# Decoder trunk on one core: gate and up slabs multiplied in two passes of 256 tokens

## The reference

```python
def swiglu(x, w_gu, w_down):
    g, u = jnp.split(x @ w_gu, 2, axis=-1)
    return (jax.nn.silu(g) * u) @ w_down

for l in range(DEPTH):          # DEPTH = 2
    x = layer_norm(ALPHA * x + 0.5 * swiglu(x, ffn1_w_gu[l], ffn1_w_down[l]), ...)
    mix = hybrid_mixer(x, positions, w_in[l], ...)   # attention, mLSTM, short convolution
    x = layer_norm(ALPHA * x + mix, ...)
    x = layer_norm(ALPHA * x + 0.5 * swiglu(x, ffn2_w_gu[l], ffn2_w_down[l]), ...)
```

## Time and profile before

| | |
|---|---|
| time, median of 2 runs | 2545.62 us (2545.02 to 2546.22) |
| span of the profiled execution | 2544.7 us |
| PE busy | 2515.7 us (99%) |
| weight loads (PEld) busy | 2053.7 us (81%) |
| DVE, ACT, POOL busy | 1131.2, 973.2, 217.8 us |
| TensorE clock granted, mean | 0.993 of full speed |
| moved by DMA | 229 MB, 90 GB/s |

### The profile page before, as it was taken

One profiled execution on the slowest core, in us unless ns is written; L12 is line 12 of the kernel. 1 busy time (PEld: TensorE's weight loads), 2 busy tenths in 40 slices (PEclk: granted clock), 3 DMA queues, 4 the chain that ended last, 5 costly groups with the idle time before them and its releaser, 6 DMA issues.

```text
span 2544.7 us, 31255 instructions
## 1 busy us (share of the span) xinstructions
PE 2515.7 (99%) x11378; PEld 2053.7 (81%) x11378; DVE 1131.2 (44%) x1584; ACT 973.2 (38%) x1334; POOL 217.8 (9%) x136
## 2 busy tenths in 40 slices
PE   8999999999999999999999999999999999999997
PEld 7888877778888778888788888787788887888886
DVE  3333344455555653333433333544455547433335
ACT  4443233344343354432344432424344433544323
POOL 0002120000000310001200021200000003000012
PEclk9999999999999999999999999989999999999999
DMA  5233232222222222322233323222222232332232
GB/s 166 90 98 99 92 88 75 77 73 83 83 83 83 96 81 89 97 95 92 95 100 99 97 92 101 55 92 67 83 83 83 68 98 83 99 99 89 90 107 79
DMA packets 229324, 229.05 MB, mean 90 GB/s; under 512 B 9440, under 2 KB 220640, under 8 KB 229216
## 3 DMA queue, kind: packets, MB, share of 16 engines
q1 hardware_dynamic: 229216, 227.66, 28.1%
HBM read 225.53 MB, written 2.10 MB: 89 GB/s over the span
## 4 chain that ended last, share of the span: by engine, by line
PE 95%; issue 2%; DVE 2%; POOL 1%; ACT 0%; DMA 0%; DVEq 0%; POOLq 0%; SPq 0%
PE main L1341 29%; PE main L1345 29%; PE main L1342 29%; PE side L1555 1%; PE side L1430 1%; DVE x L972 1%; DVE xl L966 1%; POOL ln_Q L838 1%; PE side L1377 1%; PE side L1507 1%; PE side L1541 0%; PE side L1392 0%; PE main L1372 0%; PE side L1565 0%; POOL ln_S L837 0%
## 5 line engine op out<-in xcount | busy, mean ns | idle before, releaser
L1341 PE MATMUL main<-xh,wh 128*128 128x512 f32 x2336 | 923.2, 395 | 8.7 <-ACT xh L550 7.3
L1345 PE MATMUL main<-xl,wh 128*128 128x512 f32 x2336 | 915.2, 392 | 2.1 <-DVE xl L966 1.2
L1342 PE MATMUL main<-xh,wl 128*128 128x512 f32 x2336 | 912.5, 391 | 0.0
L864 DVE TENSOR_TENSOR wl<-raw,wh 128x1024 fp32r<-128x1024 f32 (+1 forms) x443 | 538.9, 1250 | 626.6 <-ACT wh L541 619.8
L541 ACT ACTIVATE wh<-raw 128x1024 fp32r<-128x1024 f32 (+1 forms) x443 | 431.2, 1013 | 544.7 <-PE main L1345 537.1
L1341 PEld LDWEIGHTS main<-xh,wh 128*128 128x128 f32 x2336 | 440.4, 189 | 110.5 <-issue 12.2
L1345 PEld LDWEIGHTS main<-xl,wh 128*128 128x128 f32 x2336 | 440.0, 188 | 106.6 <-DVE xl L966 13.3
L1342 PEld LDWEIGHTS main<-xh,wl 128*128 128x128 f32 x2336 | 440.4, 189 | 91.3 <-issue 1.4
L1341 PE MATMUL main<-hh,wh 128*128 128x512 f32 x704 | 273.9, 389 | 0.0
L1342 PE MATMUL main<-hh,wl 128*128 128x512 f32 x704 | 273.9, 389 | 0.0
L1345 PE MATMUL main<-hl,wh 128*128 128x512 f32 x704 | 273.9, 389 | 0.0
(11 more groups left out here) (253 smaller groups left out, 2005.0 us busy)
## 6 DMA issues: line engine op xcount, KB each, us to landing
raw<-gu SPq DMA_DIRECT2D x180, 512.0 KB, 4.4
raw<-w_in SPq DMA_DIRECT2D x104, 512.0 KB, 4.5
raw<-down SPq DMA_DIRECT2D x80, 512.0 KB, 3.7
raw<-w_branch SPq DMA_DIRECT2D x24, 512.0 KB, 4.4
raw<-w_out SPq DMA_DIRECT2D x16, 512.0 KB, 4.4
raw<-w_in SPq DMA_DIRECT2D x24, 256.0 KB, 3.2
raw<-down SPq DMA_DIRECT2D x16, 256.0 KB, 3.8
x<-xT SPq DMA_DIRECT2D x4, 512.0 KB, 6.7
```

The lines of the kernel that those rows point to most:

```text
L864: ins = V.tensor_tensor(put(wl[slot]), get(raw[slot]), f32(put(wh[slot])), ALU.subtract)
L1341: T.matmul(out, hi, a, start=starts and k == 0, stop=False)
L1342: T.matmul(out, lo, a, start=False, stop=False)
L1345: ins = T.matmul(out, hi, b, start=False, stop=stops and k == kk - 1)
```

## The change

`slab` gets a parameter `parts`. With `parts=2` it goes through all rows k and halves m of the slab twice: in the first pass each product reads tokens 0 to 255 and writes the left half of its bank, in the second pass tokens 256 to 511 and the right half. Every product of 128x512 becomes two of 128x256, which lie a whole pass apart, each with its own load of the same weights. The waits stay with the first product that needs them, all in the first pass; `slab_done` is raised by the last product of the second. Only the gate and up slabs of the FFNs get `parts=2`. The down projection and the mixer are as before.

```diff
@@ -1310,7 +1310,7 @@
             def slab(layer, n, banks, rh, rl, k_first=0, starts=True, stops=True, it=None, per=0,
-                     before_k=None, before_m=None, middle=None, between=None, before_low=None):
+                     before_k=None, before_m=None, middle=None, between=None, before_low=None, parts=1):
@@ -1322,7 +1322,8 @@
                 seen = set()
-                for k, m in order:
+                wide = SEQ // parts
+                for part, (k, m) in ((p_, km) for p_ in range(parts) for km in order):
                     if (k >= kh) not in seen:
@@ -1336,11 +1337,12 @@
                     hi, lo = W[:, k, P * m:P * m + P], L_[:, k, P * m:P * m + P]
-                    out = pm[banks[m]][:, :]
-                    a, b = rh(k_first + k), rl(k_first + k)
+                    some = slice(wide * part, wide * part + wide)
+                    out = pm[banks[m]][:, some]
+                    a, b = rh(k_first + k)[:, some], rl(k_first + k)[:, some]
                     T.matmul(out, hi, a, start=starts and k == 0, stop=False)
                     T.matmul(out, lo, a, start=False, stop=False)
-                    if before_low is not None and m == ms[0]:
+                    if before_low is not None and m == ms[0] and part == 0:
                         before_low(k_first + k)
                     ins = T.matmul(out, hi, b, start=False, stop=stops and k == kk - 1)
@@ -1396,10 +1398,10 @@
                     pe.wait_ge(silu_ready.sem, silu_ready.val(layer, 22 * f) + i * 2)
-                    slab(layer, n0, (0, 1), xhk, xlk, it=i, per=2, **stream_wait(layer, 2 * f))
+                    slab(layer, n0, (0, 1), xhk, xlk, it=i, per=2, parts=2, **stream_wait(layer, 2 * f))
                     pe.wait_ge(hid_f.sem, hid_f.val(layer, 22 * f) + i * 2)
-                    slab(layer, n0 + 1, (2, 3), xhk, xlk, it=i, per=2)
+                    slab(layer, n0 + 1, (2, 3), xhk, xlk, it=i, per=2, parts=2)
```

## The result

The kernel after takes 2613.95 us (median of 2 runs, 2613.26 to 2614.64) against 2545.62: ratio 1.0268, 95% interval 1.0249 to 1.0287, so slower. The forecast was 2572 us. The time lies inside the stated range of 2548 to 2625, but far above the forecast, 5 us under rival 1's 2619.

What follows compares the result with a forecast made beforehand. PE bounds the kernel: time is number of products times pitch. Span 2544.7 + 10.6 (pitch) + 16 (FFN starts 13, clock 3) = 2571.3, median 2572 us; range 2548 to 2625, the forecast's own 2558 to 2596.

Steps and rivals of the forecast that it cites:

- rival 1: All 88 gate and up slabs: overhead is fixed per product, pitch 120.1 ns, +73 us, 2619 us; chance 0.35.
- How many: Gate and up slabs: 4224 products of 512 columns become 8448 of 256, with 8448 loads in place of 4224.
- The pitch of 256 columns: Gate and up products: 114.6 ns each, just above the load's 111.8, so two cost 2.5 ns more than one; +10.6 us.
- The two rows against rival 1: Trace rows: fp32 256-column products at 215 ns, some 2 ns overhead; fp32r 512-column products at 1.2 GHz, 0.425 us, no overhead.
- rival 2: Gate and up slabs: the load sets the pitch, 111.8 ns; -13 + 16 = +3 us, 2549 us; chance 0.08.
- rival 4: Gate and up slabs: load no longer hidden; a quarter in the open gives 140 ns and +225 us; chance 0.05.
- The first slab of an FFN: FFN starts: second pass comes behind the last row, 4.3 us later at three of four FFNs, 13 us; program start nothing.
- The clock there: Three FFN starts: clock may fall in the sparse first pass, 2 us each, 6 in all; half taken, 3 us.
- Waits that come earlier: Gate and up slabs: PE asks for the second half of low weights 2.7 us earlier; cost nothing.
- The loop's code: PE's gate and up loop: body grows from some 207 to 399 instructions and might not stay loaded.
- Rival 3: PE's loop returns: longer body not staying loaded costs 1.56 us at each of 10 x 4 returns, +62 us, 2634 us; chance 0.06.
- Sum: Whole kernel: 2544.7 + 10.6 + 16 = 2571.3 us of span, so a median of 2572 us, +1.0%.

Runs made afterwards that it cites:

- e3: The kernel after, with gate and up passes cut at 320 and 192 tokens, full loads; 2688.50 us.
- e13: e5 (bf16, 512 columns) with the numbers of xh and xl four bytes apart, weights dense; 2499.53 us.
- e14: e6 (bf16, two passes of 256) with the numbers of xh and xl four bytes apart; 2516.61 us.
- e1: The kernel after, with 64 of 128 weight columns in 5 of 6 gate and up products, rest of their output left out; 2571.34 us.
- e9: The kernel after, with 32 of 128 weight columns in 5 of 6 gate and up products, rest of their output left out; 2595.53 us.
- e8: The kernel after, with gate and up slabs in four passes of 128 tokens instead of two of 256; 5196.04 us.
- e4: The kernel after, with both halves of a product back to back in one pass, a bank's first and last product kept 512 wide; 2594.01 us.
- e7: The kernel after, with only the up slabs in two passes of 256, gate slabs as before the change; 2578.16 us.
- e10: The kernel after, with 96 of 128 weight columns in 5 of 6 gate and up products, rest of their output left out; 2582.97 us.
- e5: The kernel before, with every fp32r tile in bf16, 512 columns; 2428.95 us, ratio to before 0.9536.
- e6: The kernel after, with every fp32r tile in bf16, gate and up slabs in two passes of 256; 2450.34 us.
- e16: e6 (bf16, two passes of 256) with xh, xl and the weights wh, wl all spaced four bytes apart; 2519.65 us.
- e12: The kernel after, with passes of 384 and 128 tokens and 64 of 128 weight columns in 5 of 6 gate and up products; 2613.58 us.
- e2: The kernel before (512 tokens), with 64 of 128 weight columns in 5 of 6 gate and up products, rest of their output left out; 2558.49 us.

## Why the prediction was wrong

- **How many.** 4224 more products and loads: right.
- **The pitch of 256 columns.** Forecast 114.6, measured 120.0; this is where the forecast was lost, 45.7 us of it. The step that failed is "I take 2.5 ns fixed and the rest by the column". For this kernel's own products, fp32r with full loads, nothing goes by the column beyond 1 / 2.4 ns: the excess is 13.3 ns at 256 (after), 13.3 at 320 (e3) and 13.4 at 512 (before). With it falls the next sentence, "so the load is still hidden, with 3 ns to spare", as the reason for adding nothing for the load.
- **What the runs put in its place.** A part by the column does exist: numbers four bytes apart take 226.0 and 113.5 ns in bf16 (e13, e14), 10.1 ns over dense ones at 512 columns and 4.3 at 256. That makes 113.5, a little under the forecast. Another 6.5 ns come on top at 256 columns and only 0.7 at 512. These 6.5 ns go when the load is halved (e1, 113.3) and are partly back when it is cut to a quarter (e9, 118). So rival 1's 120.1 ns was right as a number, and its second reason, "a load and a product that both need nearly 110 ns leave little play", is a likely but not a shown one.
- **The two rows against rival 1**. Both are of other conditions, a stream of 215 ns at 2.4 GHz and one of 427 at 1.2, and were weighed too heavily. The second says less than it seems to. At the start of the kernel after, the clock being low, 256-column products stand at:

```profile
8.15 0.41 PE L1344 MATMUL main<-xh,wl 128*128 128x256 f32 x1
...
11.99 0.41 PE L1344 MATMUL main<-xh,wl 128*128 128x256 f32 x1
```

These are 18 steps in 3.84, 213.3 ns: just the columns at 1.2 GHz, and just the load's floor at that clock (e8). Two equal lengths fit together there without any excess. So the lower clock says little on the excess at the full one, and that two lengths nearly meet is not by itself the cause.

- **Rivals 2 and 4.** At 256 columns 111.8 is not reached; at 192 it is (e3). A load record still starts with each product, so the load is not in the open, as rival 4 priced it (140 ns and more). Rival 4's mechanism in a mild form, 6.5 ns, is not excluded.
- **The first slab of an FFN.** Forecast 4.3 us each, with the slab's own pitch in it, and 13 in all; measured 4.7 with the pitch, 4.1 and 12.3 without. e4 and e7 show that it goes when the halves lie together or the first slab stays whole. Right. At the program's start the FFN's gate and up loop grew by 14.15 us (241.80 to 255.95), and 22 x 48 x 13.33 ns is 14.1: no start term, as forecast.
- **The clock there.** 3 us taken for it, 0 measured: wrong, of little weight. The row it was read from was no stretch of sparse products: in the earlier trace rows it is of 8-column products, one behind the other, with PE and PEld busy throughout. In the first pass of the kernel after PE is idle for 4.4 of 14 us, and the clock stays. With passes of 128 in the same place it did fall (e8).
- **Waits that come earlier.** Right for the kernel after (1.9 us as before). In e7 a wait for low weights did appear, at layer 1's first FFN (2.1 us, at 1301), which the same argument had called nothing.
- **The loop's code.** Rival 3 refuted.
- **Sum.** 56.3 for 10.6, 12.3 for 16, and 1.8 less, unforeseen and by luck in the mixer's clock: 2544.7 + 66.8 = 2611.5 of span. The miss is the pitch, +45.7; the other two lessen it by 5.5. The lower end of the range, "rival 2 with an undisturbed clock, 2548", should have been 2546 by the prediction's own terms (-13 + 13). The measured time is in the range only because the range was drawn up to rival 1.

What stays open is why fp32r with a full load settles at 120.0 and not at 113.5. The runs show that it is not the spacing of the moving columns, not the order or the novelty of the weights, and not in proportion to the load's length. The spacing of the weights is cleared only beside the short loads of bf16. That load and product disturb each other is argued from e1 against the kernel after; e9, whose load is the shortest and whose pitch is above e1's and e10's, shows that this is not the whole of it.

## What to carry to other kernels

When an excess over the columns has to be split for a new width, rows of another type or another clock do not decide it: here they were off by 5.4 ns a product, and a small probe of that very shape would have told. For fp32r products with full loads at the full clock the price of narrower ones was 13.3 ns for each further product down to 256 columns, and at 192 the load alone set their pitch. Where a view gives a clock, check it against the pitch. Passes that are all shorter than their loads went with half the clock in e8, and doubled its time. A split in two passes also delays the end of any slab whose inputs arrive one by one by nearly one pass.

## What the runs showed of the hardware

- In bf16, a moving operand with four bytes between columns takes 226.0 ns at 512 columns and 113.5 at 256, 0.439 ns a column; with two bytes 215.9 and 109.2, 0.417 a column. Spacing the weights leaves the pitch as it is, beside load records of 0.10 us (e5, e6, e13 to e16).
- fp32r with full loads takes its columns at 2.4 GHz and 13.3 to 13.4 ns more, at 256, 320 and 512 columns (after, e3, before), and 111 to 112 at 192 (e3). At 1.2 GHz 256 columns take 213.3 with no excess (the first 12 us of the kernel after).
- 128-column fp32r products, each with a full load of its own and nothing wider between them, ran at 213.3 ns and a granted clock of 0.50 in almost all gate and up slabs and doubled the kernel's time (e8). The same products took 112 ns until the clock fell, and 111.5 with passes of 384 between (e12).
- A smaller load can make fp32r products slower: 230 for 226.7 at 512 tokens (e2), 118 for 113.3 at 256 (e9 against e1).
- bf16 in place of fp32r made the same count of products and loads 4.6% faster (e5): of the 117 us some 46 come from the gate and up slabs, 23 from the down slabs and 47 from the mixers; what DVE and ACT do faster in bf16 was not taken apart from that.
